# Norms, transposes and first weight splits woven into the chunks at three stage seams of a two-block layer kernel

## What is computed

```python
# end of layer 0 (even mixer)
y = concat([y_b, y_a]) @ w_out_e                         # stage out_e
x = layer_norm(alpha * x + gt0 * y, ln_g0, ln_b0)
# layer 1 (odd mixer); sh, sc, gt1 from modulation(c, w_ada[1])
u = x * (1 + sc) + sh
xp, gate = split(u @ w_in_o)                             # stage in_o
z = window_means(xp) - xp
z = (einsum(z, w_pool) * pool_scale)                     # stage pool, 4 groups
y = (z * silu(gate)) @ w_out_o                           # stage out_o
x = layer_norm(alpha * x + gt1 * y, ln_g1, ln_b1)
# second block
p = rms_norm_2(x, norm_mix) @ w_in_2                     # stages rkv, lora, kiwi, att4, att1
```

## Time and profile before

| | |
|---|---|
| median of 3 runs | 2770.74 us (2770.44 to 2772.83) |
| the profiled execution's own time | 2766.56 us |
| its span in the profile | 2764.8 us |
| PE busy | 2506.7 us, 91% |
| DVE busy | 1372.0 us, 50% |
| ACT busy | 1100.8 us, 40% |
| mean granted PE clock | 0.944 |

### The profile page before, as it was taken

One profiled execution on the slowest core, in us unless ns is written; L12 is line 12 of the kernel. 1 busy time (PEld: TensorE's weight loads), 2 busy tenths in 40 slices (PEclk: granted clock), 3 DMA queues, 4 the chain that ended last, 5 costly groups with the idle time before them and its releaser, 6 DMA issues. The chain is left out here.

```text
span 2764.8 us, 30528 instructions
## 1 busy us (share of the span) xinstructions
PE 2506.7 (91%) x12454; PEld 1981.6 (72%) x12454; DVE 1372.0 (50%) x1330; ACT 1100.8 (40%) x1099; POOL 44.0 (2%) x75
## 2 busy tenths in 40 slices
PE   5799999999898999796999867999789999999996
PEld 0387778886576777585888646787678888888885
DVE  0244435548636533457435597454455544545443
ACT  1444545343333333434334434234544434434332
POOL 0000000001000000000000000000000000000000
PEclk8799999999998999798999969999999999999998
DMA  9845445559944775353556001354245555555553
GB/s 394 314 154 184 139 140 177 173 184 392 368 171 147 256 261 183 139 188 124 192 167 196 16 0 40 105 204 153 93 150 185 188 191 193 188 191 190 184 197 106
DMA packets 231772, 498.72 MB, mean 180 GB/s; under 512 B 29368, under 2 KB 31416, under 8 KB 222304
## 3 DMA queue, kind: packets, MB, share of 16 engines
q1 hardware_dynamic: 224976, 459.44, 48.6%
q0 software_dynamic: 6672, 37.51, 3.6%
HBM read 493.24 MB, written 3.67 MB: 180 GB/s over the span
## 5 line engine op out<-in xcount | busy, mean ns | idle before, releaser
L1278 DVE TENSOR_TENSOR weights_lo<-weights_raw,weights_hi 128x2048 fp32r<-128x2048 f32 (+3 forms) x368 | 816.7, 2221 | 999.5 <-ACT weights_hi L676 998.3
L676 ACT ACTIVATE weights_hi<-weights_raw 128x2048 fp32r<-128x2048 f32 (+3 forms) x368 | 683.3, 1860 | 1089.5 <-PE banks L2093 1078.7
L2093 PE MATMUL banks<-weights_hi,acts_hi 128*128 128x512 f32 (+1 forms) x2336 | 928.7, 398 | 76.6 <-DVE weights_lo L1278 60.7
L2093 PE MATMUL banks<-weights_lo,acts_hi 128*128 128x512 f32 (+1 forms) x2336 | 917.7, 393 | 0.0
L2093 PE MATMUL banks<-weights_hi,acts_lo 128*128 128x512 f32 (+1 forms) x2336 | 917.3, 393 | 0.0
L2093 PEld LDWEIGHTS banks<-weights_hi,acts_hi 128*128 128x128 f32 x2336 | 446.3, 191 | 195.2 <-issue 65.6
L2093 PEld LDWEIGHTS banks<-weights_hi,acts_lo 128*128 128x128 f32 x2336 | 445.3, 191 | 93.5
L2093 PEld LDWEIGHTS banks<-weights_lo,acts_hi 128*128 128x128 f32 x2336 | 446.4, 191 | 90.9 <-issue 1.0
L2093 PE MATMUL banks<-weights_hi,hidden_hi 128*128 128x512 f32 x256 | 99.8, 390 | 0.0
L2093 PE MATMUL banks<-weights_hi,hidden_hi_odd 128*128 128x512 f32 x256 | 99.7, 389 | 0.0
L2093 PE MATMUL banks<-weights_hi,hidden_lo 128*128 128x512 f32 x256 | 99.6, 389 | 0.0
(11 more groups left out here) (484 smaller groups left out, 1959.5 us busy)
## 6 DMA issues: line engine op xcount, KB each, us to landing
raw_eight<-in_w_ada SPq DMA_DIRECT2D x80, 1024.0 KB, 16.5
weights_raw<-in_w_in_e SPq DMA_DIRECT2D x80, 1024.0 KB, 5.3
weights_raw<-in_w_up SPq DMA_DIRECT2D x64, 1024.0 KB, 5.7
weights_raw<-in_w_down SPq DMA_DIRECT2D x64, 1024.0 KB, 5.0
weights_raw<-in_w_in SPq DMA_DIRECT2D x44, 1024.0 KB, 5.1
weights_raw<-in_w_in_o SPq DMA_DIRECT2D x32, 1024.0 KB, 5.4
weights_raw<-in_w_out_e SPq DMA_DIRECT2D x16, 1024.0 KB, 5.6
gate_chunks<-in_w_ada POOLq DMA_DIRECT2D x16, 1024.0 KB, 6.4
```

The lines of the kernel that those rows point to most:

```text
L676: eng.activation(WHI[:, c % 2, :, 0:n], RAW[:, sl, :, 0:n], ACT.Copy).then_inc(hi_ready, 1)
L1278: eng.tensor_tensor(WLO[:, c % 2, :, 0:n], RAW[:, c % 4, :, 0:n], WHI[:, c % 2, :, 0:n].bitcast(F32), ALU.subtract).then_inc(lo_ready, 1)
L2093: ins = eng.matmul(BANKS[:, par * 2 + h, 0:s.n], x[:, t, h * P:(h + 1) * P], w[:, c % 2, k, 0:s.n], start=(kc == 0 and k == 0 and m == 0), ...
```

## The change

- Stages `in_o`, `out_o` and `rkv` get `ahead=2`: high and low part of their first two chunks are made in the stage before (`following`). ACT makes `hi` of the first before the last `evac`, `hi` of the second behind it; DVE makes `lo` of the first before the last block, and `lo` of the second while ACT takes the root (`rsqrt`'s `meanwhile`; at the second seam behind the last `gate_z`).
- First and third seam: PE transposes six jobs ahead of the first chunk and the last two behind it; DVE normalizes two blocks, makes jobs 0 and 1, normalizes the other two, makes jobs 2 to 5, and makes 6 and 7 behind the third `lo`. Gain and bias move behind the fifth and the sixth `lo`.
- `mod1` moves into `out_e`: PE's 32 matmuls in four steps behind chunks 6 to 9, DVE's reading behind its `lo` 9 to 13.
- Second seam: PE transposes jobs 0 and 1 of `pT` behind `pool`'s third chunk, 2 to 5 behind its fourth, 6 and 7 behind `out_o`'s first; the gate's broadcast comes behind `out_o`'s second. ACT and DVE follow.
- `rkv`: the squares move from behind `hi` 3 to behind `hi` 6, and the first block's `evac` from behind `hi` 5 to behind `hi` 7 (`late`).
- `gate_row` steps come one chunk later each. On ACT and DVE `rkv` is now written out chunk by chunk, on DVE `in_o` too; on PE two blocks of `out_o` and of `rkv` are.

```diff
-        Stage("in_o", wv(a["w_in_o"][0], 0, D, 0, NB), 8, acts="x1T", dest=lambda b, h: NATO[:, bass.ds(b, 1), h, :]),
+        Stage("in_o", wv(a["w_in_o"][0], 0, D, 0, NB), 8, acts="x1T", ahead=2, dest=lambda b, h: NATO[:, bass.ds(b, 1), h, :]),
...
-        Stage("out_o", wv(a["w_out_o"][0], 0, D, 0, NB), 4, acts="pT", dest=lambda b, h: Y[:, bass.ds(b, 1), h, :]),
-        Stage("rkv", wv(a["w_in_2"][0], 0, D, 0, NB), 6, acts="x2T", scale=0, dest=lambda b, h: NR[:, bass.ds(b, 1), h, :]),
+        Stage("out_o", wv(a["w_out_o"][0], 0, D, 0, NB), 4, acts="pT", ahead=2, dest=lambda b, h: Y[:, bass.ds(b, 1), h, :]),
+        Stage("rkv", wv(a["w_in_2"][0], 0, D, 0, NB), 6, acts="x2T", scale=0, ahead=2, late={0: 7}, dest=lambda b, h: NR[:, bass.ds(b, 1), h, :]),
...
-    GATE_AT = [(7 * m) // 4 for m in range(KT)]
+    GATE_AT = [1 + (7 * m) // 4 for m in range(KT)]
...
-        def stream(s, each=None, after=None, hold=False):
...
+        def stream(s, each=None, after=None, hold=False, following=None):
...
+                evac_at = {c + min(s.kc, 2): b for c, b in s.done.items()}
+                for b, c in s.late.items():
+                    evac_at = {k: n for k, n in evac_at.items() if n != b} | {c: b}
                 for c in range(s.nblk * s.kc):
-                    hi(s, s.g0, 0, c)
-                    b = s.done.get(c - min(s.kc, 2))
+                    if c >= s.ahead:
+                        hi(s, s.g0, 0, c)
+                    b = evac_at.get(c)
...
-            else:
-                last()
+                return
+            if following:
+                hi(following, following.g0, 0, 0)
+            last()
+            if following:
+                hi(following, following.g0, 0, 1)
...
-                                   6: lambda: gate_rows("gt0", GTB)})
+                                   6: lambda: gate_rows("gt0", GTB)}, following=st["in_o"])
...
-        eng.wait_ge(S("norm_cols"), 1)
...
-        acts_out("x1T", **norm_cols)
+
+        def normed_hi(name, n, jobs):
+            def step():
+                eng.wait_ge(S("norm_cols"), n)
+                acts_out(name, jobs=jobs, **norm_cols)
+            return step
...
-        stream(st["in_o"], after={29: gate_row})
+        stream(st["in_o"], after={1: normed_hi("x1T", 1, range(6)), 2: normed_hi("x1T", 1, (6, 7)), 29: gate_row})
...
-        stream(st["pool"])
-        acts_out("pT", scale=lambda f: cols("pool_scale", f))
-        gate_rows("gt1", GTB1)
-        stream(st["out_o"])
+        def pooled_hi(*jobs):
+            return lambda: acts_out("pT", scale=lambda f: cols("pool_scale", f), jobs=jobs)
+
+        stream(st["pool"], after={3: pooled_hi(0, 1)}, following=st["out_o"])
+        stream(st["out_o"], after={1: pooled_hi(2, 3, 4, 5), 2: pooled_hi(6, 7), 3: lambda: gate_rows("gt1", GTB1)},
+               following=st["rkv"])
...
-        eng.wait_ge(S("norm_cols"), 2)
-        acts_out("x2T", **norm_cols)
-        stream(st["rkv"], after={3: lambda: (eng.wait_ge(S("x2_done"), 1), rms_squares(XN, 0, Y))}, hold=True)
+        stream(st["rkv"], after={1: normed_hi("x2T", 2, range(6)), 2: normed_hi("x2T", 2, (6, 7)),
+                                 6: lambda: (eng.wait_ge(S("x2_done"), 1), rms_squares(XN, 0, Y))}, hold=True)
...
-                    lo(s, s.g0, 0, c)
+                    if c >= s.ahead:
+                        lo(s, s.g0, 0, c)
...
+                if following:
+                    lo(following, following.g0, 0, 0)
...
-        def rsqrt(v):
+        def rsqrt(v, meanwhile=None):
             roots[0] += 1
             ch.done("square_in")
+            if meanwhile:
+                meanwhile()
...
-            rsqrt(STAT[:, 66:71:4])
-            for b in range(4):
+            rsqrt(STAT[:, 66:71:4], lambda: lo(following, following.g0, 0, 1))
+
+        def norm_blocks(*blocks):
+            for b in blocks:
                 for h in range(2):
                     ch.add(eng.tensor_scalar(XN[:, b, h, :], XN[:, b, h, :], STAT[:, 64 + 4 * h:65 + 4 * h],
                                              STAT[:, 66 + 4 * h:67 + 4 * h], ALU.subtract, ALU.mult))
                 ch.done("block_normed")
-        def gain_bias(sem_value):
+        def normed_acts(name):
+            norm_blocks(0, 1)
+            acts_in(name, jobs=(0, 1), **norm_cols)
+            norm_blocks(2, 3)
+            acts_in(name, jobs=(2, 3, 4, 5), **norm_cols)
+
+        def gain(sem_value):
             eng.wait_ge(S("ln_in"), sem_value)
+            ch.wait()
             for h in range(2):
                 ch.add(eng.tensor_tensor(XN[:, :, h, :], XN[:, :, h, :], LNG[:, :, :], ALU.mult))
+
+        def bias():
             ch.wait()
             for h in range(2):
                 ch.add(eng.tensor_tensor(XN[:, :, h, :], XN[:, :, h, :], LNB[:, :, :], ALU.add))
+        def gain_bias(sem_value):
+            gain(sem_value)
+            bias()
+
...
-        residual_norm("gt0", st["out_e"], GTB, after={1: out_mean, 2: out_norm, 5: lambda: acts_in("yT")})
...
+        residual_norm("gt0", st["out_e"], GTB, st["in_o"],
+                      after={1: out_mean, 2: out_norm, 5: lambda: acts_in("yT"), 9: second_modulation(0),
+                             10: second_modulation(1), 11: second_modulation(2), 12: second_modulation(3),
+                             13: first_norm_cols})
...
-        acts_in("x1T", **norm_cols)
-        stream(st["in_o"], after={1: lambda: gain_bias(32)})
+        stream(st["in_o"], after={1: lambda: normed_acts("x1T"), 2: lambda: acts_in("x1T", jobs=(6, 7), **norm_cols),
...
-        stream(st["pool"], gate_z)
-        acts_in("pT", scale=lambda f: cols("pool_scale", f))
...
-        residual_norm("gt1", st["out_o"], GTB1)
+
+        def pooled_lo(*jobs):
+            return lambda: acts_in("pT", scale=lambda f: cols("pool_scale", f), jobs=jobs)
+
+        stream(st["pool"], gate_z, after={3: pooled_lo(0, 1)}, following=st["out_o"])
+        lo(st["out_o"], st["out_o"].g0, 0, 1)
+        residual_norm("gt1", st["out_o"], GTB1, st["rkv"], after={1: pooled_lo(2, 3, 4, 5), 2: pooled_lo(6, 7)})
...
-        acts_in("x2T", **norm_cols)
...
-        stream(st["rkv"], after={1: lambda: (gain_bias(64), ch.done("x2_done")), 3: lambda: inverse_rms(0)})
+        stream(st["rkv"], after={1: lambda: normed_acts("x2T"), 2: lambda: acts_in("x2T", jobs=(6, 7), **norm_cols),
+                                 4: lambda: gain(64), 5: lambda: (bias(), ch.done("x2_done")), 6: lambda: inverse_rms(0)})
...
-        stream(st["out_e"], after={3: output_tiles, 4: lambda: gate_bcast("gt0", 0)})
-        for j in range(4):
...
-            q = 32 * j
...
+        def second_modulation(j):
+            def step():
+                jj = J["mod1"] + j
...
+        stream(st["out_e"], after={3: output_tiles, 4: lambda: gate_bcast("gt0", 0), 6: second_modulation(0),
+                                   7: second_modulation(1), 8: second_modulation(2), 9: second_modulation(3)})
...
-        transposes("x1T", natural(XN), ("block_normed", 0))
+        transposes("x1T", natural(XN), ("block_normed", 0), range(6))
...
-        stream(st["in_o"], after={c: (lambda m: lambda: gate_row(m))(m) for m, c in enumerate(GATE_AT)})
+        gate_rows = {c: (lambda m: lambda: gate_row(m))(m) for m, c in enumerate(GATE_AT)}
+        stream(st["in_o"], after=gate_rows | {0: lambda: transposes("x1T", natural(XN), ("block_normed", 0), (6, 7))})
...
-        stream(st["pool"])
-        transposes("pT", natural(Y), ("gated_z", 0))
-        copied(eng, J["gate1"])
-        gate_bcast("gt1", 12)
-        stream(st["out_o"])
+        def pooled_tiles(*jobs):
+            return lambda: transposes("pT", natural(Y), ("gated_z", 0), jobs)
+
+        def second_gate():
+            copied(eng, J["gate1"])
+            gate_bcast("gt1", 12)
+
+        stream(st["pool"], after={2: pooled_tiles(0, 1), 3: pooled_tiles(2, 3, 4, 5)})
+        stream(st["out_o"], after={0: pooled_tiles(6, 7), 1: second_gate})
...
-        transposes("x2T", natural(XN), ("block_normed", 4))
+        transposes("x2T", natural(XN), ("block_normed", 4), range(6))
...
-        for n in ("rkv", "lora", "kiwi"):
-            stream(st[n])
+        stream(st["rkv"], after={0: lambda: transposes("x2T", natural(XN), ("block_normed", 4), (6, 7))})
```

More of the change, by code:

```diff
@@ L127, in __init__ @@
         self.turned = turned
+        self.ahead = ahead
+        self.late = late or {}
         self.rot = rot
@@ L1585, in each @@
                     ch.add(eng.bn_stats(STAT[:, h * 32 + 6 * b:h * 32 + 6 * b + 6], XN[:, b, h, :]))
-            stream(s, each, after=after)
+            stream(s, each, after=after, following=following)
             ch.wait()
```

61 lines of the change are left out of this document (35 added, 26 removed).

## The result

The changed kernel takes 2751.82 us (median of 4; 2743.45 to 2753.06) against 2770.59 (four executions; the three of the prediction gave 2770.74), a ratio of 0.9927 (95% interval 0.9904 to 0.995): 18.8 us faster, where 26.9 were forecast. On another chip, measured side by side, it was 2751.61 against 2771.95, 20.3 less. The profiled execution took 2743.45, 23.1 less than the profiled one before. The time lies in the range, above the likeliest case's own 2739 to 2749. Two things need an explanation: what is missing at the seams, and why the medians gain less than the two profiled executions.

What follows compares the result with a forecast made beforehand. PE was taken to bound the stages, the chain through ACT and DVE the seams. Gains of 14.2 (second seam), 6.5 (first) and 6.2 (third) sum to 26.9 us, from 2770.74 to 2743.9; range 2737 to 2757.

Steps and rivals of the forecast that it cites:

- likeliest case: Whole kernel: the forecast itself, 2743.9 us, with 2739 to 2749 as its own range; chance 0.66.
- PE bounds the stages, the chain through ACT and DVE the seams: Between 780 and 1330 us: PE sets the pace within a stage, 5.44 us a chunk; ACT and DVE bound the seams.
- Second seam, 14.2: pool to out_o: pool's end to out_o's fourth chunk's end takes 26.7 us instead of 40.9, gaining 14.2.
- First and third seam, the common part: With T the last chunk's end before the seam: first chunk begins at T + 18.5, second ends at T + 32.5.
- First seam, 6.5: out_e to in_o: gap gains 11.2 us, mod1 inside out_e costs 4.7, leaving a gain of 6.5.
- 64 / 15 = 4.3: mod1 in out_e: 64 passes at 15 a us, full clock, cost 4.3 us.
- 9.1: mod1 in out_e: upper bound of its cost in us, 64 passes at 7 a us, half clock.
- Rival A: PE pays more for the clock, at mod1's steps and at first chunks: gain 12 to 18, about 2756 us; chance 0.13.
- rival B: Woven transposes and high parts wait for one another, 0.6 us for each of 12: about 2751 us; chance 0.15.
- C: As a rival: slower, engines wait for code in the written-out streams, about 2792 us at 3 a chunk; chance 0.03.
- D: As a rival: no effect, 2770 us, only if out_e grew by what the seam gives; chance 0.03.
- 6.2: Third seam, into rkv: gap gains 8.5 us, 2.3 given back by waits behind it, leaving 6.2.

Runs made afterwards that it cites:

- the second trace: The changed kernel profiled once more, no edit; median 2751.6 us.
- seam_two_undone: Changed kernel with the second seam put back as before (all of pT between pool and out_o, no weights ahead): 2761.9 us.

## Why the prediction was right, and where it was not

- *PE bounds the stages, the chain through ACT and DVE the seams.* Right: distances between chunk ends inside the stages did not move, and all of the gain lies in B, E and F (D did not change).
- *Second seam, 14.2.* Measured 15.1 in D + E, 13.4 by undoing it alone; the forecast lies between. No piece of `pT` made PE wait.
- *First and third seam, the common part.* The first chunk came at T + 17.8 where 18.5 stood, the second chunk ended at T + 30.9 and 31.4, where 32.5 stood. Behind the third seam 2.4 us were given back (G), 2.3 forecast.
- *First seam, 6.5.* Wrong, and this is the step that failed. The gap gained 12.9 (226.1 less 213.2 in B + C), not 11.2; but `mod1` cost 11.5, and 10 in the second trace, against 4.7. The seam brought 1.4 to 2.3. The mis-sized term is "64 / 15 = 4.3": the window's x15 counts records that touch the microsecond, those of two overlapping trains and those that only end in it. The group's own row, 7.52 us for 64 passes, part of them at half clock, should have warned; the spacing of the steps gives 0.111 a pass at full clock. The x7 of the low rate is misread in the same way, so 9.1 was no upper bound: the last twelve passes of that train start 0.213 us apart at half clock, which makes 13.6 of 64. The rule of the Trainium skill that I set aside for that row ("TensorE: Matmul & The Clock Gate", "LDWEIGHTS (loading the stationary operand)") makes 107 ns of a load of 128 columns; the measured 111 agrees with it, and its sum of 6.8 for the passes is close to the 7.1 of 64 times 0.111. The change from chunks to a step and back was put at 0.1 and costs 0.31, and 1.6 to 3.1 went to the clock.
- *Rival A, the clock.* It was right in part: behind one or two of the four steps the clock fell with PE busy for 1.00, and the rule from "What's actually happening" on the same page of the Trainium skill, by which the busy steps could not drop it, does not agree with these windows, if busy means what the profile's rows count. The other half of A, a first chunk wholly at half clock, did not come.
- *Rivals B, C and D.* No piece at the second seam waited for another (B); the waits shown above have none by "issue" (C); `out_e` grew by 11.5, a third of the 35 that the three gaps gave (D asked for all of it).
- *The sum.* 26.9 forecast; 14.2 became 15.1, 6.5 became 1.4, 6.2 became 7.1: 23.6 by stretches. H took 3.0 back. That is the clock: over all 14 traces H goes with the time at half clock in it, 75.1 us before and 78.5 in seam_two_undone, where H is 235; 88.7 in the changed kernel and the three others with 238 or 239; 92 to 96 where it is 241; 96 to 106 where it is 243 or more. One place beside 1745 is between 1526 and 1531 of the changed kernel, with a clock of 0.71, where the same work before had 1.00. Why the changed kernel's H is about 3 us longer in both pairs of traces is open: nothing was run that shifts the clock alone.
- *What was luck.* The two other seams brought 0.9 more each than forecast, which hides 1.8 of the 5.1 that the first seam missed. And 2751.8 is the time that rival B named, though nothing that B describes happened: the range held it because it was wide enough for B.

## What to carry to other kernels

Make the first weights of a stage while the last chunks of the one before still run: alone it brought 12 us at the fourth seam, and at the first and third the split of the activations was only some 2 of the 9.5 to 12.9 us that the gaps gave. Fill an idle gap before moving work out of it: here 64 passes beside DVE's statistics made the seam 0.7 to 1.3 us longer, and in a full stream they cost their whole length and dips of the clock, 10 to 11.5 us. When pieces are woven between chunks, add up the chain from one chunk's end to the chunk that needs it, pieces and weight split together, against what the bounding engine has left to do.

## What was not expected of the hardware

- The granted clock fell in the middle of uninterrupted TensorE work: behind one or two of four trains of 16 one-column passes (3.4 us at half clock each time, 1.6 us lost), not behind trains of 8 (one trace), and for 20.5 us in all with trains of 32 (one trace).
- The same program's same stretch took 235.2 or 241.4 us; 6.0 of the 6.2 us come from one place, where the clock was at half for 3.4 or 20.5 us around a pause of 3.2 us, in the second case for over 15 us with PE busy again. Medians can hide differences of 5 us between kernels whose traces show them plainly.
